# Splitting the mixer of a hybrid decoder layer into three token blocks, two of them interleaved with the expert gathers

## What is computed

```python
# x <- LN1(alpha*x + Mixer(x));   x <- LN2(alpha*x + PEER(x))
def _mixer(x, ...):
    proj = x @ w_in                      # 1024 -> 2048 columns
    # 512 columns: causal conv of 4 -> gated linear recurrence over time -> * gelu(gate)
    # 256 columns: B * conv3(C * x_sc)
    # 256 columns: softmax attention into 256 memory tokens
    # RMSNorm of each group, then one output projection
    return concat(...) @ w_out
def _peer(x, wq, keys, u_tab, v_tab):    # per token
    qb = x @ wq                          # 8 heads x 2 halves x 128
    v1, i1 = top_k(qb1 @ keys1, 16); v2, i2 = top_k(qb2 @ keys2, 16)
    top_s, e = top 16 of the 256 sums v1+v2         # 16 expert numbers out of 16384
    g = softmax(top_s)
    act = gelu(x . u_tab[e])             # 8 heads x 16 experts
    return sum(g * act * v_tab[e])
```

## Time and profile before

| | |
|---|---|
| median of 3 executions | 3400.89 us |
| the profiled execution, its own time | 3404.87 us |
| its span, first to last instruction | 3403.0 us |
| granted TensorE clock, mean | 0.799 of full speed |
| TensorE busy | 2607.5 us, 77% |
| VectorE busy | 2134.4 us, 63% |
| ScalarE busy | 1320.1 us, 39% |
| GpSimd busy | 1151.2 us, 34% |
| moved by DMA | 1209.03 MB, 355 GB/s over the span |

### The profile page before, as it was taken

How to read it: one execution, slowest core, us unless ns; L and a number is a source line. 1 busy time by engine, 2 the same in 40 slices (tenths; PEclk the granted TensorE clock), 3 DMA queues, 4 the chain that set the end, 5 groups by cost and what they waited for, 6 DMA issues and landing times.

```text
span 3403.0 us, 37868 instructions
## 1 busy us (share of the span) xinstructions
PE 2607.5 (77%) x11476; PEld 944.3 (28%) x11476; DVE 2134.4 (63%) x4722; ACT 1320.1 (39%) x3873; POOL 1151.2 (34%) x1092
## 2 busy tenths in 40 slices
PE   8989898888777767767777777777677778866766
PEld 4665444233322222222222221222122224410010
DVE  1453646778866676667666766676666665565454
ACT  1432102554444444444444444344434433343343
POOL 0000002444443444444444444443444443343342
PEclk9989998878877787887777777778877776677677
DMA  5001155999999999999999999999999997899998
GB/s 191 19 19 74 63 198 226 421 398 408 415 421 421 421 404 422 416 412 409 421 419 404 414 416 421 421 405 416 421 405 413 418 421 303 319 421 421 421 421 333
DMA packets 175261, 1209.03 MB, mean 355 GB/s; under 512 B 19792, under 2 KB 23120, under 8 KB 34768
## 3 DMA queue, kind: packets, MB, share of 16 engines
q0 software_dynamic: 156672, 1140.92, 81.5%
q1 hardware_dynamic: 18384, 65.68, 5.2%
HBM read 1192.02 MB, written 14.51 MB: 355 GB/s over the span
## 4 chain that ended last, share of the span: by engine, by line
issue 41%; POOL 25%; PE 20%; DMA 6%; DVE 5%; ACT 2%; POOLq 0%; SPq 0%; DVEq 0%; ACTq 0%
POOL arena L444 25%; PE ps L481 7%; DMA arena<-in_uv,idxT 6%; PE ps L620 4%; PE ps L721 3%; DVE arena L1327 2%; PE ps L655 2%; PE ps L705 1%; PE ps L670 1%; PE ps L497 0%; PE ps L525 0%; PE ps L459 0%; PE ps L536 0%; POOLq L442 0%; PE ps L515 0%
## 5 line engine op out<-in xcount | busy, mean ns | idle before, releaser
L721 PE MATMUL ps<-arena,wset 128*32 128x512 f32 x4352 | 1460.5, 798 | 695.2 <-ACT wset L955 622.7
L444 POOL DMA_INDIRECT arena<-in_uv,idxT x1088 | 1151.0, 1058 | 2223.7 <-PE ps L721 1580.5
L1327 DVE CUSTOM_DVE_ANT_0 arena<-arena 128x1024 f32<-128x1024 f32 x1088 | 1331.2, 1225 | 911.0 <-DMA arena<-in_uv,idxT 843.9
L946 ACT ACTIVATE gel<-acts 128x1 f32<-128x1 f32 x1088 | 219.8, 202 | 1395.3 <-DVE acts L1327 1382.5
L721 PEld LDWEIGHTS ps<-arena,wset 128*32 128x32 f32 x4352 | 187.9, 123 | 1735.1 <-ACT wset L955 1512.1
L955 ACT ACTIVATE wset<-arena,wt 128x32 f32<-128x32 f32 x1088 | 349.5, 321 | 54.2 <-PE ps L721 18.4
L950 ACT ACTIVATE wt<-gel,gT 128x1 f32<-128x1 f32 x1088 | 320.4, 294 | 103.1 <-ACT gel L946 3.4
L655 PEld LDWEIGHTS ps<-arena 128*128 128x128 f32 x2304 | 315.2, 220 | 124.5 <-issue 124.5
L655 PE MATMUL ps<-arena 128*128 128x128 f32 (+1 forms) x2304 | 340.4, 310 | 0.7 <-issue 0.7
L705 PE MATMUL ps<-arena 32*128 32x512 f32 x704 | 265.7, 839 | 5.3 <-ACT arena L925 3.8
L481 PE MATMUL ps<-arena 128*128 128x384 f32 (+1 forms) x768 | 247.4, 481 | 0.7 <-ACT arena L835 0.7
(11 more groups left out here) (154 smaller groups left out, 1408.6 us busy)
## 6 DMA issues: line engine op xcount, KB each, us to landing
arena<-in_uv,idxT POOLq DMA_INDIRECT x1088
arena<-in_w_in SPq DMA_DIRECT2D x16, 512.0 KB, 3.5
arena<-in_x_tok SPq DMA_DIRECT2D x9, 512.0 KB, 4.8
scratch_x<-arena SPq DMA_DIRECT2D x9, 512.0 KB, 3.0
scratch_x1T<-arena SPq DMA_DIRECT2D x9, 512.0 KB, 2.6
arena<-scratch_x1T SPq DMA_DIRECT2D x9, 512.0 KB, 4.3
arena<-in_w_out SPq DMA_DIRECT2D x1, 4096.0 KB, 13.2
arena<-in_xT SPq DMA_DIRECT2D x2, 1536.0 KB, 13.8
```

Source lines behind the costliest of these rows:

```text
L444: pool.indirect_dma_start(out=ring[n % RING], out_offset=None, in_=A["uv"], in_offset=bass.IndirectOffsetOnAxis(ap=idxT[t % 2][:, col:col ...
L721: last = mm(ps[r0:r0 + 32, hf * HALF:(hf + 1) * HALF], wset[n % SETS][:, :], v[:, hf * HALF:(hf + 1) * HALF], start=first, stop=final)
L946: A_(gel[:, n % COLS:n % COLS + 1], acts[:, n % COLS:n % COLS + 1], ACT.Gelu).then_inc(gelus, 1)
L1327: V.tensor_tensor_reduce(out=ring[n % RING][:, 0:D], in0=ring[n % RING][:, 0:D], in1=xrep[g % 2], scale=1.0, scalar=0.0, op0=ALU.mult, op1 ...
```

## The change

The mixer is done in three token blocks (tiles 0 to 2, 3 to 5, 6 to 8). Only the first block runs ahead of the expert stage, with its output projection and LayerNorm. The gathers of tile 0 begin when the first unit of tile 0 is chosen. All work of blocks 1 and 2 is cut into pieces. A table `PLAN` names for each engine the piece and the slot at which it begins, and `stepper` runs pieces between the slots at a pace given in `PE_PACE` and `DVE_PACE`. The state of the recurrence and of the convolutions is carried from block to block (`hcar`, `carry`, `carry2`).

SBUF holds the ring from the start, so neither all of `wq` nor all of `w_in` fits beside it. Every weight piece (512 KB) is streamed through three buffers `win`, once for each block. `x1T` no longer goes through DRAM. The queries are computed for a whole block at a time, stored to DRAM (`scratch_q`, 256 KB for each unit) and loaded one unit at a time ahead of `keyscores`. The windows of tile 3 become 16 slots each and begin at slot 320.

```diff
+BLOCKS = [(0, 384, 384, 3), (384, 384, 384, 3), (768, 256, 320, 3)]
+LEAD = -200
+BASE = [LEAD, 76, 384]
 def window(u):
...
+    if t == 3:
+        return 320 + 16 * k, 16
     return 128 * (t - 1) + 32 * k, 32
+def plan_later_block(b):
+    o = BASE[b]
+    put("sp", o - 6, b, "xT")
+    for i, (name, c) in enumerate(PROJ):
+        put("pe", o + 8 * i, b, "half", (name, c))
+        put("pe", o + 8 * i + 4, b, name, c)
+        put("act", o + 8 * i + 6, b, name, c)
+    for c in range(CL):
+        x = o + 16 * c
+        put("dve", x + 25, b, "cv", c)
+        put("pe", x + 31, b, "gr", c)
+        put("act", x + 31, b, "sr", c)
...
+        put("act", x + 33, b, "ta", c)
+        put("dve", x + 34, b, "ra", c)
+        put("act", x + 39, b, "sd", c)
+        put("dve", x + 40, b, "re", c)
...
+    plan_queries(b, o + 219, 4)
+def plan_queries(b, x, each):
+    for side in range(SIDES):
+        put("pe", x + each * side, b, "wq", side)
+        put("act", x + each * (side + 1), b, "we", side)
+        if side % 4 == 3:
+            put("sp", x + each * (side + 1) + 1, b, "sq", side // 4)
...
+    for side in range(8, SIDES):
+        put("pe", 9 + 2 * (side - 8), "w0", side)
...
+    plan_queries(0, 26, 3)
+PE_PACE = {"half": 0.5, "oq": 1, "wq": 0.5, "w0": 0.25, "xt": 0.25, "nm": 0.25, "ss": 0.25, "sv": 0.25}
+DVE_PACE = {"ra": 1, "no": 1, "l2": 1, "mx": 0, "nz": 0, "ty": 0, "q2": 0}
+def stepper(entries, run, pace):
...
+            if next(state[1], "end") == "end":
+                state[0], state[1] = state[0] + 1, None
+            elif n >= 0:
+                state[2] += pace(*entries[state[0]][1:3])
     def _(sp):
+        def weight(i):
+            if i >= WIN:
+                after(sp, "pe", *W_USE[i - WIN][1:])
...
+        def load_q(u):
...
+            load(ld_q[u % 2], qTb[u % 2], O["q"][t, :, k, :])
     def _(pool):
-        pool.wait_ge(op_mm, NL)
         for n in range(NSLOT):
...
+            if n == 4:
+                after(pool, "pe", 0, "op", (2, 1))
     def _(pe):
...
         for n in range(NSLOT):
...
-                if at == window(u)[1] // 4 and u + 1 < NUNIT:
-                    q_gen = query(u + 1)
-                next(q_gen, None)
...
             if n >= 1:
                 combine(n - 1)
+            mix(n)
```

More of the change, by code:

```diff
@@ L26 @@
 SIDES = 2 * PH
-SLOTS = PH * TOPK
 TILES = SEQ // P
@@ new lines @@
+plan_first_block()
+plan_later_block(1)
+plan_later_block(2)
+for _e in ("pe", "act", "dve"):
+    PLAN[_e].sort(key=lambda x: x[0])
+STREAMED = {"oq", "wq", "w0", "ss", "sv"} | {n for n, _ in PROJ}
+_began = {(b, *a): s for s, b, n, a in PLAN["pe"] if n == "half"}
+W_USE = sorted([(_began.get((b, n, a), s), b, n, a) for s, b, n, a in PLAN["pe"] if n in STREAMED],
+               key=lambda x: x[0])
+for _i in range(len(W_USE)):
+    PLAN["sp"].append((LEAD - 1 if _i < WIN else W_USE[_i - WIN + 1][0], W_USE[_i][1], "win", _i))
@@ L127, in sb @@
         return t.__enter__()
[L130 to L141, removed]
@@ L154, in build @@
[L154 to L165, removed]
@@ L181, in build @@
[L181 to L190, removed]
+    TM = 392
+    a = Carver(sb("arena", [P, 50552])[:, :], 0)
+    ring = [a.take(2 * D) for _ in range(RING)]
@@ new lines, in _ @@
+        for v in range(LEAD, LEAD + 20):
+            mix(v)
+        load("wout", w_out, A["w_out"])
+        load("ln", ln_v, A["ln"].partition_broadcast(P))
+        load("keys", keysT, A["keys"])
+        load("sel", sel, A["sel"])
+        for v in range(LEAD + 20, 0):
+            mix(v)
+        q_at = {max(window(u)[0] - 6, window(u - 1)[0] + 1): u for u in range(4, NUNIT)}
+        s1_at = {3 * b + ti: s for s, b, name, ti in PLAN["sp"] if name == "s1"}
+        x1_at = {max(TILE_END[t - 2] + 5, s1_at[t] + 3): t for t in range(2, TILES + 1)}
@@ new lines, in _ @@
+        for n in range(NSLOT):
+            mix(n)
+            if n in q_at:
+                load_q(q_at[n])
+            if n == 20:
+                load_x1(1)
+            t = SLOT[n][0]
+            if n in x1_at:
+                sp.wait_ge(res_done, x1_at[n] - 1)
+                load_x1(x1_at[n])
+            if t >= 1 and n - TILE_END[t - 1] == FINISH + 8:
+                sp.wait_ge(yo_ready, t)
+                store_y(t - 1)
+        after(sp, "dve", 2, "sh", CS - 1)
+        sp.dma_start(O["states"], st[:, :]).then_inc(st_state, 16)
@@ L629, in _ @@
[L629 to L658 removed]
+        holder = {}
@@ new lines, in claim, with landed, project @@
+        def claim(k, who, b, name, arg=0):
+            if k in holder:
+                after(pe, *holder[k])
+            holder[k] = (who, b, name, arg)
+            return bank[k]
+        def landed(b, name, arg):
+            i = W_AT[(b, name, arg)]
+            pe.wait_ge(ld_win[i % WIN], 16 * (i // WIN + 1))
+            return win[i % WIN]
+        def project(b, name, c, k0, k1, out_):
+            w_ = landed(b, name, c).rearrange("p (k m) -> p k m", k=KD)
+            x_ = x8(zone1, b)
+            for kk in range(k0, k1):
+                last = mm(out_, w_[:, kk, :], x_[:, kk, :], start=kk == 0, stop=kk == KD - 1)
+                if kk == KD - 1:
+                    last.then_inc(stage["pe"], 1)
+                yield
@@ L723, in combine @@
             last.then_inc(used, 1)
[L725 to L739 removed]
+        sqb = {6: xc0, 7: xc1, 0: gg0, 1: gg1, 2: gg2, 3: rb, 4: ib0, 5: ib1}
+        mix = stepper(PLAN["pe"], run, lambda b, name: 0.33 if (b, name) == (0, "wq") else PE_PACE.get(name, 0))
+        for v in range(LEAD, 0):
+            mix(v)
+        u = 0
         for n in range(NSLOT):
```

1507 lines of the change are left out of this document (841 added, 666 removed).

## The result

| | before | after |
|---|---|---|
| median of the runs | 3393.13 us (3384.06 to 3402.91, 4 runs) | 3269.5 us (3269.15 to 3270.41, 4 runs) |
| ratio to before | | 0.9636, 95% interval 0.9601 to 0.967 |
| span of the profiled execution | 3403.0 us | 3267.3 us |
| first gather, last gather | 554.8, 3374.0 us | 212.1, 3236.3 us |
| from the first to the last | 2819.2 us | 3024.2 us |

What follows compares the result with a forecast made beforehand. Bound by the lead (555 us before the first gather), then by DMA gathers at 421 GB/s (2710 us). Span 3403 - 335 + 215 - 44 + 25 = 3264 us, so 3262 us measured; range 3195 to 3365 us.

Steps and rivals of the forecast that it cites:

- Term 1: Before the first gather: the lead holds a third of the mixer, first gather at 220 us, -335 us.
- C: In the lead: in-order engines wait for each other; first gather at 285 us, total 3327 us; chance 0.07.
- Term 2: Expert stage: the gathers themselves do not change, 2710 us for 1088 slots.
- Term 3: SyncE's transfers after the first gather: 77.6 MB more cost +215 us, bounds 184 and 419 us.
- Term 4: 2800 to 2960 us: the slow stretch goes, since the last tile's queries are made within block 2; -44 us.
- Term 5: Block work between slots on VectorE and ScalarE fits, but stacked delays run the DMA queue dry; +25 us, bounds 0 and 100.
- Six more like it at 4 us: Where delays outlast the ring's cover: six more cases like TensorE's 6.08 us wait at a tile end, 4 us each.
- No stretch below 370: Sign of being right: from the first gather to the end 405 to 421 GB/s, no stretch below 370.
- A: Slots 26 to 667: added transfers cost 5.4 us per MB, 419 us, total 3441 us, slower; chance 0.10.
- B: Mixed stretches: TensorE binds at a clock of 0.72, +140 us for 25, total 3377 us; chance 0.10.
- above 0.85: Sign of being right: TensorE's clock in the mixed stretches stays above 0.85.
- D: Tile 3: queries stored at slot 312, wanted at 320, come ten slots late; gathers stop 30 us, total 3292 us; chance 0.04.

Runs made afterwards that it cites:

- the best complete version: Both gate sigmoids computed as `tanh` and the four `sv` pieces spread over 12 slots, against the changed kernel: 3242.01 us, 27 us under it.

## Why the prediction was right, and where it was not

**What bounds the kernel** held: the lead, then the gathers at 421 GB/s.

**Term 1, the lead** (-335, measured -343): the first gather came at 212.1 us for 220. Of the 8 us, 6 lie in the block itself: its last norm product ended at 149 us for the forecast's 155, though TensorE was busy 128 of the 149 us, 86%, about the share that was chosen. What was too large is the work that was divided by it: the 132 us were summed from groups of lines, and consecutive products overlap in them (in this lead the groups sum to 134 us where TensorE was busy 128). The chain behind it took 63 us for 65. C falls. The 3 us charged for `op` ahead of the choice did not show: the run that moved `op` has its first gather at 211.4 us, and the price of the order lies at the fifth and ninth gathers.

**Term 2, the gathers** (0): 1088 of them, and 421 GB/s wherever the queue is full.

**Term 3, the traffic** (+215, 189.5 by the full rate): this step was mis-sized. The amount was right, 122.32 MB for 122 in all and 79.8 for 77.6 added behind the first gather. The price for weights, 2.38 us per MB, was an upper value (2.0 with the holes filled). The 1.65 us per MB for rows of 2 KB, read from two stretches of the earlier trace rows at 401 and 388 GB/s, measured 0.3. Those stretches lay at tile ends, and what they lacked was not the rows' price but that of the other work there; this last is argued, only the 0.3 is measured, and for DRAM-to-DRAM rows. The difference is about 25 us.

**Term 4, the dip of the last tile** (-44): 420 GB/s where it was 304. It went as said.

**Term 5, the work between the slots** (+25, measured about +60): this step failed, though the value lies within its bounds of 0 to 100. "Six more like it at 4 us" took one wait at a tile end as the pattern. The runs show in its place three stretches in which the delays stack for 120 to 160 us: 27 us from table switches (and returns), 11 from the `sv` loads in a ring of three, and in the first dip VectorE behind the switches. That leaves some 22 us. "No stretch below 370" was wrong: 338, 350 and, at 240 to 280 us, just 370. ScalarE's total was estimated well and was no guide: it was busy 95.82 of 160 us in the worst stretch. Its switches were counted well too: 55 with their returns are 140 us, and the run without them has 93 loads less, 119 us. What failed is the step from "it fits" to a cost: each delay was held to be covered by the ring but for six. Of the 60 us the best complete version took back 27. Of the rest some is VectorE's, and how much was not settled.

Terms 3 and 5 were off by 25 and 35 us in opposite directions, so that 3262 for 3269.5 is closer than the working deserved: that much of it is luck. (The lower end of the range, 3195, does not come out of the bounds given for it either: a lead of 197 and a price of 184 us make 3208. Nothing turned on it.)

**Rivals.** A (5.4 us per MB): 2.0 measured for added traffic, and even with every added stall charged to it the change's own traffic cost (205.0 + 44.5) / 79.8 = 3.1 us per MB, under the 4.9 that decides; it falls. The Trainium skill's rule ("DMA: Bandwidth & Descriptors", section "Anatomy of one DMA — SWDGE (gpsimd) path"), 2.0 us plus the bytes for each DMA, is fitted for GpSimd's path; put on SyncE's 105 transfers of 0.52 MB, it would by an estimate have made them cost 336 us if nothing overlapped. The trace doesn't agree that it may be added up: 108 us. B (TensorE binds at 0.72): the clock in the mixed stretches was 0.83 to 1.00, and where TensorE was busy 118.75 of 120 us the DMA engines still moved 419 GB/s. It falls, but by the small margin that was forecast. By "TensorE: Matmul & The Clock Gate", section "What's actually happening" of the Trainium skill, activity releases the throttle, and these rows agree: 0.73 at 107.78 of 160 us busy, 1.00 at 118.75 of 120. The sign "above 0.85" was missed in the third dip, 0.83. D falls: behind the first gather GpSimd waited for a choice (`idxT`) only three times, 219.4 - 211.7 = 7.7 us in all, and 1040 to 1240 us, with the first choices of tile 3 in it, is at 418 GB/s.

## What to carry to other kernels

Fill a stage that is bound by DMA with the work of the lead, and price the new traffic by its bytes at the rate that the full stage shows; then look for the cost not in any engine's total but in the places where two kinds of extra work fall between the same slots. An engine that is busy 60% of the time can hold the queue under its rate for 160 us when the chain from one buffer to the next runs through it and each link gets a delay: put activation functions that share a table together, and space the loads that share a small ring. When a stage starts, look at when each buffer of its ring comes free, and when the first one is given back, not only at its first transfer.

## What the runs showed of the hardware

- Added DRAM-to-DRAM traffic (55 MB) beside a full gather queue moved at no loss where the queue was full: 422 GB/s between 1120 and 1280 us. Halving its rows from 4 to 2 KB cost 0.3 us per MB.
- `tanh` and `gelu` ran without a table load between them (in the changed kernel `gelu` at 566.72, `tanh` at 567.65, `gelu` again at 568.15 us), while sigmoid, square root and exp each loaded one (1.28 us) and `gelu` one more behind them. Sigmoid written as `tanh` removed 31 loads of 196 and 13 us. The Trainium skill ("ScalarE: Activation LUTs", section "Table sets: the hidden batching unit") says to batch activations by the set that they share, and the run agrees. The section puts a load at about 2.7 us, which is the page's figure for a load with the drain behind it (section "What ACT_TABLE_LOAD costs"); here a load took 1.28, and near 603 us the next instruction began 0.01 us behind it.
- The removal of one load of 1.28 us was worth 0.4 us (31 loads, 13 us), and of all in the blocks 0.3 us (93 loads, 27 us). The rest of their 1.28 us did not show in the time; that the ring covers it is argued, not shown.
- VectorE's reciprocal took 2.55 us for 384 columns, 6.6 ns a column, where a product of two tensors took 0.55.
